# A transformer block with a two-branch mixer, cross-attention, a conv FFN, a second mixer and a routed mixture of experts: squares summed before the matmul, new orders in the second mixer and the router, four loads from ScalarE's queue, all up units on unscaled input, a reordered beginning

## The reference, cut to what matters

```python
# first block
h = rms_norm(x, norm_mix_pre); proj = h @ w_in          # q, k, v, u, gates
o_attn, o_ssm = stick_breaking_attention(q, k, v), s5_branch(u, ...)
merged = gate_attn * (o_attn @ w_branch_attn) + gate_ssm * (o_ssm @ w_branch_ssm)
x = x + rms_norm(merged @ w_out, norm_mix_post)
x = x + rms_norm(memory_cross_attention(rms_norm(x, norm_xa_pre), rms_norm(mem, norm_mem), ...), norm_xa_post)
x = x + rms_norm(conv_ffn(rms_norm(x, norm_ffn_pre), ...), norm_ffn_post)   # d_ff = 2816, gelu(gate) * val
# second block
x = x + hybrid_mixer(rms_norm_2(x, norm1), ...)         # mLSTM heads (q, k, v, o) beside a gated MLP (u, v) with spatial mixing
x = x + moe(rms_norm_2(x, norm2), ...)                  # 4 groups x 8 experts, top 2, d_ff 512
y = rms_norm_2(x, final_g)
```

## Time and profile before

| | |
|---|---|
| runs | 1215.39, 1209.56, 1210.02 us, median 1210.02 |
| profiled execution | 1210.39 us; its span 1208.6 us |
| PE busy | 1118.3 us (93%) x6998, mean granted clock 0.961 |
| DVE busy | 642.1 us (53%) x1367 |
| ACT busy | 406.1 us (34%) x693 |
| HBM read | 300.39 MB, 249 GB/s over the span |
| chain that ended last | PE 80%, DVE 10%, ACT 4%, DMA 4%, issue 2% |

### The profile page before, as it was taken

How to read it: one execution, slowest core, us unless ns; L and a number is a source line. 1 busy time by engine, 2 the same in 40 slices (tenths; PEclk the granted TensorE clock), 3 DMA queues, 4 the chain that set the end, 5 groups by cost and what they waited for, 6 DMA issues and landing times.

```text
span 1208.6 us, 17666 instructions
## 1 busy us (share of the span) xinstructions
PE 1118.3 (93%) x6998; PEld 842.8 (70%) x6998; DVE 642.1 (53%) x1367; ACT 406.1 (34%) x693; POOL 10.1 (1%) x28
## 2 busy tenths in 40 slices
PE   8899999999987999996988886999999999999995
PEld 5888778968987999996787785444455444444442
DVE  5999996645468787876677544222222222222213
ACT  5413255444444565655564221111111111111112
POOL 1000000000001000000000000000000000000000
PEclk9999999999968999998998897999999999999998
DMA  7444333443323666653333259999999999999994
GB/s 275 146 160 140 96 104 125 157 150 110 121 72 124 209 212 225 213 188 107 122 122 105 70 199 412 406 420 421 422 420 420 422 422 420 421 422 420 421 420 175
DMA packets 55780, 302.62 MB, mean 250 GB/s; under 512 B 6400, under 2 KB 6544, under 8 KB 31120
## 3 DMA queue, kind: packets, MB, share of 16 engines
q1 hardware_dynamic: 54576, 297.03, 64.0%
q10 hardware_dynamic: 720, 3.33, 0.7%
q0 software_dynamic: 400, 1.10, 0.3%
HBM read 300.39 MB, written 1.05 MB: 249 GB/s over the span
## 4 chain that ended last, share of the span: by engine, by line
PE 80%; DVE 10%; ACT 4%; DMA 4%; issue 2%; ACTq 0%; SPq 0%; DVEq 0%
PE psum L1848 79%; DVE arena L1070 2%; DMA sq<-in_experts 2%; DVE w_low L1070 2%; DVE arena L1073 2%; DMA ring<-in_stream 1%; ACT arena L1024 1%; DVE rt L1073 1%; ACT w_high L632 1%; PE psum L2503 1%; DVE h L1073 1%; DVE h_low L1070 0%; DMA arena<-in_memT 0%; DVE rstd L1073 0%; DVE arena L1066 0%
## 5 line engine op out<-in xcount | busy, mean ns | idle before, releaser
L1848 PE MATMUL psum<-arena 128*64 128x512 f32 (+5 forms) x1520 | 275.1, 458 | 10.8 <-ACT arena L1024 5.3
L1848 PEld LDWEIGHTS psum<-arena 128*64 128x64 f32 (+2 forms) x1520 | 152.6, 161 | 133.0 <-issue 126.2
L1848 PE MATMUL psum<-h_high,w_high 128*128 128x256 f32 x672 | 196.9, 293 | 9.2 <-DVE w_low L1070 5.7
L1070 DVE TENSOR_TENSOR w_low<-ring,w_high 128x1024 fp32r<-128x1024 f32 x146 | 176.7, 1221 | 33.1 <-ACT w_high L632 32.5
L1848 PE MATMUL psum<-h_low,w_high 128*128 128x256 f32 x672 | 194.1, 289 | 0.0
L1848 PE MATMUL psum<-h_high,w_low 128*128 128x256 f32 x672 | 193.8, 288 | 0.0
L632 ACT CAST w_high<-ring 128x1024 fp32r<-128x1024 f32 x146 | 151.3, 1045 | 44.5 <-DMA ring<-in_stream 32.0
L1848 PEld LDWEIGHTS psum<-h_high,w_high 128*128 128x128 f32 x672 | 133.1, 198 | 13.3 <-issue 9.8
L1848 PEld LDWEIGHTS psum<-h_low,w_high 128*128 128x128 f32 x672 | 133.2, 198 | 0.3 <-issue 0.2
L1848 PEld LDWEIGHTS psum<-h_high,w_low 128*128 128x128 f32 x672 | 133.0, 198 | 0.0
L1073 DVE SCALAR_TENSOR_TENSOR arena<-arena,psum 128x512 f32<-128x512 f32 (+1 forms) x44 | 29.1, 662 | 190.7 <-ACT arena L1020 183.2
(11 more groups left out here) (263 smaller groups left out, 1458.3 us busy)
## 6 DMA issues: line engine op xcount, KB each, us to landing
arena<-in_experts SPq DMA_DIRECT2D x99, 1024.0 KB, 22.5
ring<-in_stream SPq DMA_DIRECT2D x180, 512.0 KB, 3.5
parts<-in_experts SPq DMA_DIRECT2D x30, 1024.0 KB, 25.4
ring<-in_experts SPq DMA_DIRECT2D x30, 1024.0 KB, 26.1
sq<-in_experts SPq DMA_DIRECT2D x10, 1024.0 KB, 22.6
h<-in_experts SPq DMA_DIRECT2D x10, 1024.0 KB, 23.4
x<-in_experts SPq DMA_DIRECT2D x10, 1024.0 KB, 24.3
arena<-in_experts ACTq DMA_DIRECT2D x3, 1024.0 KB, 5.7
```

The costliest lines, as they stand in the source:

```text
L1070: return dve.tensor_tensor(o, a, b, op)
L1848: return pe.matmul(o, a, b, start=start, stop=stop, skip_group_check=True)
```

## The change

It has seven parts.

1. `rsqrt`: one step makes the seed, two dependent steps refine it, one Newton step follows (6 dependent steps for 8).
2. Beginning: ACT squares one column of `ones` before the first real square and waits for `cols` only behind that square; DVE splits q 0 ahead of `norm_scale(1)`, and the next four units one place later each.
3. Norms 5 and 7 take squares added by DVE (`squares_added`), norm 6 squares of tiles 0 to 5 added by DVE; PE sums them in one place, not between the units. `add_gained` makes its first pair of tiles one by one. DVE splits v2 0, 1, 2 around norm 6, not before it, and masks `mixw` behind norm 7.
4. FFN: every pass takes the unscaled input; `scaled_up(j)` stands first in each pass of DVE, ACT's copy and `normed_split(5)` are gone; hidden tiles go to `hh`/`hl`.
5. Second mixer: o2 0 ahead of the transposes and decay rows, `mix` ahead of the qk2 pairs, values 0 and 1 ahead of qk2 pair 3, out2 units 4 and 5 split in parts like 0 to 3; orders of ACT and DVE to match. Squares go to memory of their own (`gm_sq`, `hm_sq`, `headed32`).
6. Router: token sums from squares of `x` by PE, not from the turned rows; half of the turns behind the logits; 12 and 4 matmuls whose result is not used around the ranks.
7. Loads 16, 17, 7 and 8 are issued by ACT: at norm 7, at the gate rows, and both last behind o2 1. In the expert loop the scatter moves behind the transposes of `hx`.

```diff
+                link(ts(y.bitcast(I32), a.bitcast(I32), -0.5, ALU.mult, RSQRT_SEED, ALU.add))
+                weighed_square()
+                link(stt(t, t, 5 * RSQRT_GAIN ** 2 / 3, t, ALU.add, ALU.mult))
+                link(stt(y, t, 5 * RSQRT_GAIN ** 4 / 4, y, ALU.add, ALU.mult))
+                weighed_square()
+                return stt(y, t, 1.5, y, ALU.add, ALU.mult)
...
-            for s in range(3, 9):
-                if s == 7:
-                    sp.wait_ge(used, UNIT_AT["o2", 3] + 1)
-                sp.dma_start(held[s], experts[s]).then_inc(expert_in[s], 16)
-            for s in (16, 17):
+            for s in range(3, 7):
                 sp.dma_start(held[s], experts[s]).then_inc(expert_in[s], 16)
...
+            act.wait_ge(consts, 1)
+            link(act.activation(msq[:, 0, 0:1], ones[:, 0:1], ACT.Square))
             memory_tiles(0)
...
-                if j >= UNSCALED:
-                    act.copy(up[:, b, :, 4:4 + T], bank[:].rearrange("p (c t) -> p c t", c=2))
-                if j == 0:
-                    operand_high(hh, h, KT)
...
             act.wait_ge(scales, 8)
+            act.dma_start(held[16], dram["experts"][16]).then_inc(expert_in[16], 16)
...
             qk_gate(3)
             decayed(2)
             decayed(3)
+            weights_high(UNIT_AT["out2", 2] + 1)
             evict_o(1)
+            for s in (7, 8):
+                act.dma_start(held[s], dram["experts"][s]).then_inc(expert_in[s], 16)
...
-            weights_low("u", 3)
+            weights_low("q", 0)
             norm_scale(1)
...
+            squares_added(5)
+            weights_low("fg", 2)
             norm_scale(5)
-            weights_low("fg", 2)
             scaled_up(0)
-            normed_split(5, rms=rb[:])
-            weights_low("fv", 2)
             for j in range(FT):
                 b = j % 3
+                if j:
+                    scaled_up(j)
                 if j + 1 < FT:
                     weights_low("fv", j + 1)
...
+            weights_low("v2", 1)
+            norm_scale(6)
+            weights_low("v2", 2)
+            add_gained(6, "dn", "norm1", yh, yl, 16)
+            squares_added(7)
+            weights_low("vg", 1)
+            norm_scale(7)
...
+            weighted(0)
+            weighted(1)
+            operand_lows(yh, yl, headed32, headed, range(4, 8), op_low)
             convolved(2)
             weights_low("o2", 3)
             gated_qk(2)
+            gated(0)
+            gated(1)
             weights_low("out2", 0)
             convolved(3)
...
-                            if j == 0 and c == 0 and k % 2:
-                                norm_sum(5, k // 2)
-                    if j == 0:
-                        norm_spread(5)
+                        if j == 0 and c == 1:
+                            pe.wait_ge(halved, 3)
+                            halved_sums(STAT, sq)
+                        if j == 1 and c == 0:
+                            norm_spread(5)
...
+            cols_pair("o2", 0)
             xb.claim(pe, ("gT", 0))
...
             decay_rows(1)
-            cols_pair("o2", 0)
-            cols_pair("qk2", 0)
             pe.wait_ge(vn_ready, 2)
...
+            cols_pair("qk2", 0)
             cols_pair("qk2", 2)
             head_sums(0)
...
-            cols_pair("qk2", 3)
             head_values(0)
             head_values(1)
+            cols_pair("qk2", 3)
...
+            for _ in range(12):
+                mm(dbank[1][:, 0:P], ident[:], ones[:], True, True)
             xb.claim(pe, ("rank", 0))
             pe.wait_ge(sel_ready, 1)
...
-                    if p:
-                        scatter(0)
-                        scatter(1)
                     pe.wait_ge(hx_ready, total(r, PAIRS, p + 1))
                     for f in range(FE // P):
                         ins = pe.transpose(psum[4][:, f * P:f * P + P], hx[:, f * P:f * P + P], ident[:])
                     ins.then_inc(hT_done, 1)
+                    if p:
+                        scatter(0)
+                        scatter(1)
```

294 lines of the change are left out of this document (158 added, 136 removed).

## The result

The changed kernel takes **1166.67 us** (median of 4 runs, 1165.84 to 1167.33), against 1210.12 for the kernel before in the same comparison: a ratio of 0.9625, 95% interval 0.9603 to 0.9648. The forecast was 1172, range 1160 to 1190. The profiled execution took 1166.3 us, its span (first to last instruction) is 1164.6.

A forecast was written before the change was run, and what follows sets the result against it. The end was taken to hang on when the uninterrupted, DMA-bound stream of expert loads starts and how many loads were already issued. Terms 26.6 + 10.0 + 2.6 - 1.3 = 37.9 us off gave 1172 us, range 1160 to 1190.

The forecast's parts named there:

- Start of the stream: The moment SP's uninterrupted expert loads begin: 26.6 us earlier, at 683.3 for 709.9, summed over all stages ahead of it.
- Beginning: Kernel start up to k 2: earlier table load 0.6 us, shorter `rsqrt` 0.4 us twice; 1.4 us off.
- Norm 4 to FFN pass 3: FFN entry: norm sums leave PE's order and `rsqrt` shortens; 8.3 us off despite a new 3.5 us wait at fv 2.
- rival 3: FFN passes: DVE, not PE, sets the pace, a pass may take 9.3 us, total 1186 us; chance 0.06.
- Second mixer: From the end of `if` to the stream's start: reordering saves 14.9 us, with 4 us set against it for half clock.
- Four loads: Expert loads 16, 17, 7, 8 issued early by ACT: 12 loads follow the stream's start, not 16; 10.0 us less.
- Standstill: DMA's idle time before the first used expert buffer is refilled: 1 to 2 us, not 4; 2.6 us off.
- Scatter: Expert loop, scatter behind the transposes: no gain in the middle, last pair's down units 1.7 us later.
- 1 (mixer's waits return): Second mixer: its waits come back elsewhere, 8 to 10 of the 14.9 us go, about 1181 us; chance 0.17.
- 2 (early loads give nothing): Expert loads: early issue gains nothing, by the queue rule or a late router; costs 12.6 us, 1185 us; chance 0.08.
- 4, slower: FFN passes: DVE work covers none of ACT's steps, a pass takes 11.6 us, total 1234 us; chance 0.03.
- rival 5: Better than forecast: no half clock in the mixer and none at FFN entry, 1162 us; chance 0.04.

The follow-up runs named there:

- b_rsqrt: The kernel before with the new `rsqrt` alone: 1204.83 us, ratio 0.9941 to the kernel before.
- a_table_old: The changed kernel with ACT's table load back behind the landing of the constants, no early dummy square: 1165.86 us.
- b_front: The kernel before with only the change's beginning, `rsqrt`, DVE-added squares, unscaled up units and new order of norms 6 and 7; old mixer, router, loads and scatter: 1189.03 us.
- a_late: The changed kernel with 100 spare matmuls behind the router's ranks in place of 4, to delay the first use of an expert: 1184.95 us.
- b_again: The kernel before, unchanged, run once more for a second trace: 1215.79 us.
- b_nudge: The kernel before with 13 in place of 10 rounds of spare matmuls at the very start, nothing else: 1213.2 us, ratio 0.9997.
- a_no_spare: The changed kernel without the 12 and 4 spare matmuls in the router: 1169.46 us.

## Why the prediction was right, and where it was not

**The bound and its one moment.** Right, and the strongest part: in all fourteen traces the last gate/up unit comes a fixed time behind S, 460.3 to 461.1 or 471.6 to 471.8 us by the number of loads still to bring, unless the first unit comes behind the cover.

**Start of the stream**: forecast 26.6 us earlier, measured 35.7. The difference of 9.1 is close to what b_rsqrt shows without the rest of the change (8.8); measured against it, S came 701.17 - 674.24 = 26.9 earlier. That is one trace each, and S of the seven kernels with this FFN and this mixer order lies between 674.24 and 678.79, a spread of 4.5 us that no edit explains. What the prediction had wrong is "`rsqrt` loses two of its 8 steps of 0.2 us, 0.4 us" together with "a pass takes 8.64 us on PE": one of the two steps takes 0.39, so it is 0.6 us at each norm, and in every trace with that edit but one the matmuls of 256 columns follow 1.3 to 2.7 ns sooner in the FFN. No row before could show the latter. By its own terms:
- *Beginning*, 1.4: did not come. Measured 0.4 later at k 2. Half of the term was the table load, which a_table_old shows to be worth nothing; DVE's added squares are late next, and PE runs at half clock behind that wait. That norm 4 is spread 1.2 us earlier all the same, close to the 1.3 forecast up to there, is luck: b_rsqrt alone has 2.5.
- *Norm 4 to FFN pass 3*, 8.3 with the 0.4 of `rsqrt`: 9.9 with the 0.6 (9.3 without), and the new wait of 3.5 at fv 2 came as 3.73. Fg 0 got three waits of 0.34 to 0.42 for DVE's low parts in place of the sums.
- *FFN passes*, nothing and 0.2 once: DVE didn't become the bound, rival 3 is out (DVE is busy 145 of 160.5 us; the forecast of 7.6 in a pass is 7.65). The 3.7 us gained are the slot.
- *Norm 6 to `if`*, 6.1: 7.9 (v2 0 starts 17.6 us behind the end of the FFN passes, before 21.2).
- *Second mixer*, 14.9 less 4: 13.7, or 13.0 against b_front and 10.3 against b_rsqrt. The 4 us set aside for stretches at half clock were about right: the mean clock is 0.96 over 89.2 us, which makes some 3.6 (an estimate). What came on top is of the size of b_rsqrt's gain in the old mixer, 3.4.

**Four loads**, 10.0: right in mechanism and size (10.7). **Standstill**, 2.6: there was none to win; the cover with 16 loads reaches to about 43 us, and the kernel before was inside it with 42.3. The term's arithmetic put the end of DMA's work at 42.1 us behind S (32.1 with 12 loads) and the moment at which data flow again 3.9 us behind the first unit. The traces put the first at some 44.5 (before) and 35 (a_late), and data flow again some 2 us behind the first unit (a_late: 724.92 and about 727). So each was off by 2 to 3 us, both made the standstill too long, and the 4 us were not lost. But b_again and b_nudge, whose routers were slower at 48.7 and 45.9, did stand still: part of the scatter of the kernel before's runs is this.

**Scatter**: forecast +1.7 in the tail, less 0.4 by `rsqrt`; measured +2.4. Its price is 1.4 at full clock and 3.2 at half. That the middle would not gain from it was right.

**Router**: first use forecast 29.1 us behind the start, measured 28.8, the gather 3.8 us for 3.2. As to the spare matmuls, the trace of a_no_spare says that they only hold the margin.

**The sum** came out 6.1 us short of the measured 44.0 by three errors: 9.1 too little ahead of the stream, 1.9 too much behind it (12.6 for 10.7), 1.1 too little loss in the tail. The range had room for a term that nobody had forecast; that the result stayed in it owes something to luck. Of the signs named, two failed: the first expert load came at 674 and not near 683, a pass took 8.44 and not 8.64.

**Rivals.** 1 (mixer's waits return) showed on a small scale, at values 2, as forecast. 2 (early loads give nothing) is false as the kernel stands and true with a late router. 4, slower, was never near: a pass of 10.4 us or more against 8.44. That 1166.7 lies between the forecast and rival 5 has mainly another cause than the clock rival 5 named: `rsqrt` and the slot.

## What to carry to other kernels

Find the moment from which one resource is full to the end, and count in what each edit moves that moment and how much work is left behind it; gains ahead of it arrive as far as no wait for another engine takes them up (in b_front 11.0 of 13.8 us), and while one resource is full, work saved on another engine behind that moment doesn't arrive, except in the tail. Moving loads ahead of that moment takes their time off whatever queue issues them, but it also shortens the cover for the step that hands back the first buffer, so the two have to be shortened together. When a wait is taken out by splitting something earlier, look at the next unit that the same engine has to prepare: here it moved from fv 2 to dn 0 and cost as much there.

## What the runs showed that I had not expected

- In the FFN the mean distance of matmuls of 256 columns took one of three values, 117.3, 118.7 or 120.0 ns, constant over a stretch of 160 us at a granted clock of 1.00. It was 120.0 in all three traces with the old `rsqrt`; the difference is 3.7 us in the FFN alone. With the new one it differed from kernel to kernel. The spread of b_rsqrt's runs (9.6 us) is no evidence for it: the kernel before, with the same router, spread by 10.1 over 11 runs.
- 2.2 us of idleness ahead of the last transposes cost another 1.7 us by the clock in four of seven traces of kernels with the same tail, and nothing in three.
- A spare matmul of 128 columns in plain float took 0.23 us as two records, twice what I had read from one row.
